# First feed-forward lifted from the unscaled h, S5 parameters moved, 64-row scores in the NSA attention

## The reference

```python
def first_block(...):
    for l in range(DEPTH):
        h = h + hybrid_mixer(rms_norm(h, norm_mix[l]), ...)
        h = h + memory_cross_attention(rms_norm(h, norm_xattn[l]), mem, ...)
    return rms_norm(h, norm_final)          # x * rsqrt(mean(x * x) + eps) * g

def second_block(x, ...):
    h = x
    h = h + 0.5 * _swiglu(_rmsnorm(h, ffn1_norm[0]), ffn1_w_in[0], ffn1_w_out[0])
    ...                                     # S5, feed-forward, kv, feed-forward
    logits = q @ k * 64 ** -0.5 + bias      # NSA: 16 heads of 64, per head and branch
```

## Time and profile before

| | us |
|---|---|
| median of 3 runs | 1496.9 (1495.55 to 1497.25) |
| the profiled execution | 1496.62 |
| its span, first to last instruction | 1494.9 |
| PE busy | 1412.1 (94%) |
| VectorE busy | 845.7 (57%) |
| ScalarE busy | 808.2 (54%) |
| GpSimd busy | 327.3 (22%) |
| chain that ended last | 83% PE, 7% VectorE, 4% ScalarE, 3% GpSimd |

### The profile page before, as it was taken

How to read it: one execution, slowest core, us unless ns; L and a number is a source line. 1 busy time by engine, 2 the same in 40 slices (tenths; PEclk the granted TensorE clock), 3 DMA queues, 4 the chain that set the end, 5 groups by cost and what they waited for, 6 DMA issues and landing times.

```text
span 1494.9 us, 21758 instructions
## 1 busy us (share of the span) xinstructions
PE 1412.1 (94%) x7242; PEld 1165.2 (78%) x7242; DVE 845.7 (57%) x1240; ACT 808.2 (54%) x1322; POOL 327.3 (22%) x369
## 2 busy tenths in 40 slices
PE   7998989999879999958999999999999989999998
PEld 6887878887758887747778888888888875788887
DVE  6537665447566545645665555555555568555553
ACT  7676566665665555322654444765444548464442
POOL 2011000011169979836230000010000015000000
PEclk9999999999989999957999999999999969999999
DMA  9522635513356564210676665577656320355661
GB/s 332 172 91 72 225 128 182 155 58 109 105 145 207 173 176 142 70 29 15 222 245 190 188 187 187 162 146 223 194 182 195 120 71 2 113 183 182 194 185 57
DMA packets 170925, 224.71 MB, mean 150 GB/s; under 512 B 15881, under 2 KB 113393, under 8 KB 170849
## 3 DMA queue, kind: packets, MB, share of 16 engines
q1 hardware_dynamic: 168016, 217.27, 45.8%
q0 software_dynamic: 2160, 6.02, 2.5%
q10 hardware_dynamic: 672, 0.42, 0.1%
HBM read 221.16 MB, written 1.44 MB: 149 GB/s over the span
## 4 chain that ended last, share of the span: by engine, by line
PE 83%; DVE 7%; ACT 4%; POOL 3%; issue 2%; SPq 0%; DMA 0%; ACTq 0%; POOLq 0%; DVEq 0%
PE psum L1611 14%; PE psum L1599 10%; PE psum L1601 10%; PE psum L1600 10%; PE psum L386 8%; PE psum L388 8%; PE psum L387 8%; PE psum L412 2%; PE psum L520 2%; DVE w_lo L338 1%; PE psum L1638 1%; POOL w_raw L2019 1%; PE psum L534 1%; PE psum L2753 1%; ACT w_hi L330 1%
## 5 line engine op out<-in xcount | busy, mean ns | idle before, releaser
L1798 DVE TENSOR_TENSOR w_lo<-w_raw,w_hi 128x1024 fp32r<-128x1024 f32 x216 | 278.3, 1290 | 290.0 <-ACT w_hi L1732 289.8
L1732 ACT ACTIVATE w_hi<-w_raw 128x1024 fp32r<-128x1024 f32 x216 | 228.7, 1060 | 307.4 <-PE psum L1601 216.8
L338 DVE TENSOR_TENSOR w_lo<-w_raw,w_hi 128x1024 fp32r<-128x1024 f32 (+4 forms) x191 | 225.4, 1207 | 121.1 <-ACT w_hi L330 119.6
L1599 PE MATMUL psum<-w_hi,x_hi 128*128 128x512 f32 x704 | 280.9, 399 | 1.5 <-DVE x_lo L438 0.7
L1601 PE MATMUL psum<-w_hi,x_lo 128*128 128x512 f32 x704 | 275.7, 392 | 0.0
L1600 PE MATMUL psum<-w_lo,x_hi 128*128 128x512 f32 x704 | 275.1, 391 | 0.0
L330 ACT ACTIVATE w_hi<-w_raw 128x1024 fp32r<-128x1024 f32 (+4 forms) x191 | 193.3, 1038 | 107.0 <-PE psum L388 61.0
L386 PE MATMUL psum<-w_hi,x_hi 128*128 128x512 f32 (+5 forms) x608 | 232.2, 382 | 3.7 <-DVE x_lo L2886 2.3
L388 PE MATMUL psum<-w_hi,x_lo 128*128 128x512 f32 (+5 forms) x608 | 227.6, 374 | 0.0
L387 PE MATMUL psum<-w_lo,x_hi 128*128 128x512 f32 (+5 forms) x608 | 227.1, 374 | 0.0
L1601 PEld LDWEIGHTS psum<-w_hi,x_lo 128*128 128x128 f32 x704 | 132.7, 188 | 28.6
(11 more groups left out here) (407 smaller groups left out, 1835.4 us busy)
## 6 DMA issues: line engine op xcount, KB each, us to landing
w_raw<-in_ffn_w_in SPq DMA_DIRECT2D x352, 256.0 KB, 3.2
w_raw<-in_ffn_w_out SPq DMA_DIRECT2D x176, 256.0 KB, 2.9
w_raw<-in_w_in SPq DMA_DIRECT2D x88, 256.0 KB, 3.4
w_raw<-in_w_out SPq DMA_DIRECT2D x32, 256.0 KB, 3.8
w_raw<-in_w_kv SPq DMA_DIRECT2D x24, 256.0 KB, 2.9
w_raw<-in_mem_wk SPq DMA_DIRECT2D x16, 256.0 KB, 5.7
w_raw<-in_mem_wv SPq DMA_DIRECT2D x16, 256.0 KB, 4.9
w_raw<-in_mem_wq SPq DMA_DIRECT2D x16, 256.0 KB, 6.6
```

Source lines behind the costliest of these rows:

```text
L338: nc.vector.tensor_tensor(w_lo[:, s, 0:size(u)], w_raw[:, s, 0:size(u)], w_hi[:, s, 0:size(u)].bitcast(F32), ALU.subtract).then_inc(lo_rea ...
L1599: nc.tensor.matmul(o, xh, whi, start=(kt == 0), stop=False)
L1732: nc.scalar.activation(w_hi[:, s, :], w_raw[:, s, :], ACT.Copy).then_inc(hi_ready, 1)
L1798: nc.vector.tensor_tensor(w_lo[:, s, :], w_raw[:, s, :], w_hi[:, s, :].bitcast(F32), ALU.subtract).then_inc(lo_ready, 1)
```

## The change

1. The first feed-forward lifts the unscaled `h`. Its column factor becomes the product of both weights (`norm_final` comes a second time as rows of 8 x 128, is turned by PE and multiplied into `ffn1_norm`), its row factor the product of both `rstd` (`ffn0.scale`). Pairs 0 and 1 are lifted inside `wo1.1`, as soon as the first residual half is there. The final scaling of `h` moves behind the lifts of pairs 2 and 3; the feed-forward's own norm is still taken from the scaled `h`.
2. The S5 activations move to the end of the mixer and the reciprocal to the start of `dve_mem`; GpSimd loads B and C after the values of the memory attention.
3. The NSA scores of a job are two matmuls of 64 rows, one for each head, into the two score banks; the zeros in `kTz` are no longer needed. The compressed scores use the T banks.

```diff
-        nf = area("nf", D)
+        nf = area("nf", D, at=areas["mix"][0])
+        nf_rows = area("nf_rows", P)
...
         def pe_scores(pe, tag, j, job):
-            b = take(pe, "S", f"{tag}.s{j}")
+            banks = [take(pe, "S", x) for x in score_banks(tag, j, job)]
...
+            for i in range(2):
+                o = psum[:, pools["S"][i], 0:job["nk"]] if job["by_rows"] else psum[:, banks[0], i * SEQ:i * SEQ + job["nk"]]
+                last = nc.tensor.matmul(o, job["q"][i], job["k"][i], start=True, stop=True)
...
@@ act_mixer
+            if l == DEPTH - 1:
+                act_s5_params(act)
             for f in range(2):
                 hi_parts(act, chunk_start(f"out{l}.1") + f + 2 + RING)
                 act_lift(act, f"memq{l}", KT, gcol[f"norm_xattn{l}"], pairs=[f])
+            if l == DEPTH - 1:
+                act_s5_params_2(act)
...
@@ pe_mem
+            if l == DEPTH - 1:
+                pe.wait_ge(loads["final"], 32)
+                b = take(pe, "T", "final.gb")
+                nc.tensor.transpose(psum[:, b, 0:KT], nf_rows[0:KT, :], ident[0:KT, 0:KT]).then_inc(*done("lift_pe", "final.gain_turned"))
...
-                for c in range(2):
-                    pe_chunk(pe, f"wo{l}.{c}", tiles_first=None if c else f"mem{l}.olo")
+                pe_chunk(pe, f"wo{l}.0", tiles_first=f"mem{l}.olo")
+                pe_chunk(pe, f"wo{l}.1", after={2: lambda: pe_ffn_lift(pe, 0, [0]), 4: lambda: pe_ffn_lift(pe, 0, [1])})
...
@@ act_mem
-                act_s5_params_2(act)
+                act.wait_ge(*when("final.gain"))
+                for f in range(2):
+                    hi_parts(act, chunk_start(f"wo{l}.1") + f + RING)
+                    act_lift(act, "ffx0", KT, ffn_gain(0), pairs=[f])
+                return
...
@@ dve_mem
+            if l == DEPTH - 1:
+                dve_s5_reciprocal(dve)
...
-                lo_parts(dve, chunk_end(f"wo{l}.0"))
-                dve_s5_reciprocal(dve)
-                dve_residual(dve, f"mem{l}", [f"wo{l}.0", f"wo{l}.1"])
+                def lift_half():
+                    for f in range(2):
+                        lo_parts(dve, chunk_start(f"wo{l}.1") + f + RING)
+                        dve_lift(dve, "ffx0", KT, ffn_gain(0), pairs=[f])
+
+                lo_parts(dve, chunk_end(f"wo{l}.1") + 1)
+                dve.wait_ge(*when("final.gain"))
+                dve_residual(dve, f"mem{l}", [f"wo{l}.0", f"wo{l}.1"], before={1: lift_half}, convert=False)
...
@@ dve_final
-            dve_norm(dve, "final", 20)
             dve.wait_ge(*when("final.rstd"))
-            dve.wait_ge(loads["final"], 16)
+            dve.wait_ge(*when("ffx0.turned3"))
+            dve.wait_ge(loads["final"], 32)
...
@@ act_ffn
-                act_norm(act, f"ffn{f}", i, [FFN_AFTER[f] + ".h11"], [FFN_JUNK[f]])
-                act.wait_ge(*when(f"ffn{f}.rstd"))
+                act_norm(act, f"ffn{f}", i, ["final.h11" if f == 0 else FFN_AFTER[f] + ".h11"], [FFN_JUNK[f]])
+                act.wait_ge(*when("ffn0.scale" if f == 0 else f"ffn{f}.rstd"))
...
@@ dve_ffn
             dve_lift(dve, f"ffx{f}", KT, ffn_gain(f), pairs=range(lifted, KT // 2))
+            if lifted_hook:
+                lifted_hook()
...
+            if f == 0:
+                nc.vector.tensor_tensor(rstd[:, i:i + 2], rstd[:, i:i + 2], rstd[:, 20:22], ALU.mult
+                                        ).then_inc(*done("norm_dve", "ffn0.scale"))
...
@@ pool_s5
-            pool.wait_ge(*when("final.h11"))
+            pool.wait_ge(*when("mem1.sm.pv3"))
...
@@ pool_kv
-            step(nc.gpsimd.memset(kTz, 0.0), "nsa.kTz0")
...
@@ nsa_jobs
-                            q=[qT[:, a, t * P:(t + 1) * P]], k=[kTz[:, NKV * br + a // 2, :, 0:nk]],
+                            q=[qT[HD * i:HD * i + HD, a, t * P:(t + 1) * P] for i in range(2)],
+                            k=[kTz[HD * i:HD * i + HD, NKV * br + a // 2, i, 0:nk] for i in range(2)], by_rows=True,
...
@@ pe_nsa
-                b = take(pe, "S", f"cmp.scores{t}")
+                b = take(pe, "T", f"cmp.scores{t}")
...
@@ sync
+            sp.dma_start(nf_rows[0:KT, :], d["norm_final"].rearrange("(k p) -> k p", p=P)).then_inc(loads["final"], 16)
...
@@ the queues' ends
-            pe_ffn(pe, 0, hooks=...
+            pe_ffn(pe, 0, lifted=2, hooks=...
...
-            dve_final(dve)
-            dve_ffn(dve, 0, hooks=...
+            dve_norm(dve, "final", 20)
+            dve_ffn(dve, 0, lifted=2, lifted_hook=lambda: dve_final(dve), hooks=...
```

More of the change, by code:

```diff
@@ L1491, in dve_mem @@
             dve.wait_ge(*when(f"mem_scale{l}.1"))
+            if l == DEPTH - 1:
+                dve.wait_ge(*when("final.gain_turned"))
+                nc.vector.tensor_tensor(ffn_gain(0), ffn_gain(0), bank("final.gb")[:, 0:KT], ALU.mult
+                                        ).then_inc(*done("norm_dve", "final.gain", frees=("final.gb",)))
             lo_parts(dve, chunk_end(f"wq{l}.0"))
@@ L1767, in act_ffn, with dve_ffn @@
             hi_parts(act, ahead(12))
[L1769 removed]
+        def dve_ffn(dve, f, first=None, early=None, lifted=0, hooks={}, next_lift=None, next_weights=True, in_tail=None, lifted_hook=None):
             u0 = ffn_first[f]
@@ L1776, in dve_ffn @@
                 dve.wait_ge(*when(f"ffn{f}.rstd"))
+            if f == 0:
+                nc.vector.tensor_tensor(rstd[:, i:i + 2], rstd[:, i:i + 2], rstd[:, 20:22], ALU.mult
+                                        ).then_inc(*done("norm_dve", "ffn0.scale"))
+                dve.wait_ge(*when("ffn0.scale"))
             def hidden(c):
```

35 lines of the change are left out of this document (14 added, 21 removed).

## The result

The changed kernel takes 1487.57 us in the median of four runs (1485.51 to 1489.45), the kernel before 1497.08 beside it: 9.5 us less, a ratio of 0.9942, 95% interval 0.9921 to 0.9963. In a second comparison on another chip it was 1486.37 against 1495.23, ratio 0.9930 (0.9908 to 0.9953). The ratios are not the quotients of the medians: by them the change gives 8.7 and 10.5 us, by the medians 9.5 and 8.9. The forecast was 1484.4, 12.5 us less, in a range of 1480.5 to 1490.5. The profiled execution of after took 1487.92, its span is 1486.2.

A forecast was written before the change was run, and what follows sets the result against it. The prediction took the matmul engine, busy for 94% of the span, as the bound. Final norm 7.7 plus scores 4.8 made 12.5 us, so 1496.9 - 12.5 = 1484.4, range 1480.5 to 1490.5.

The forecast's parts named there:

- A delay below 2.6 us is free; 3 us more would pass on: First weights of the next chunk (`u0+4`), beside B and C loads: landing 415.5, needed 418.1; further delay reaches the second residual.
- rival A: Final norm gives only 3 to 4 us of 7.7, through a long dip or late `u0+4`; 1489, chance 0.16.
- The dip: Clock at half speed after PE's 3.2 us gap before the first feed-forward matmuls: loses 1.7 us, bounds none to 2.8.
- The end still moves by 7.7: End of the S5 stage: GpSimd's tables gain only 5.2 us, but its slack lets the end gain the full 7.7.
- that slack: GpSimd's 3.11 us idle for VectorE at the stage's end, 0.6 left after the change; losing it costs up to 1 us.
- Scores: NSA attention, paired 64-row halves: 4.3 us from t = 1, 0.9 from t = 0, less 0.4 at the start; 4.8.
- The estimate from the Trainium skill's page: NSA scores: 1.5 times for two row tiles instead of 1.9, a block of 0.71 and a gain of 3.3 us.
- B: NSA scores: 64-row halves don't pair, so that part gives 0 to -1.5 us; 1489.5, chance 0.15.
- C: NSA scores: 64-row matmuls neither pair nor hide weight loads, +21 us over 32 jobs; 1505, chance 0.05.
- D: Final norm: norm, squares and root bind `f_hid`, PE ends where it was; 1492 with scores only, or 1497; chance 0.04.
- E: Both parts give more: no dip, attention intervals set by ScalarE, 9.4 + 6.2 us; 1481.3, chance 0.10.
- the moved steps: S5 activations and reciprocal in mixer and memory attention: taken as 0, up to 2 us on `memq1` without cover.

The follow-up runs named there:

- e6_params_old: Changed kernel with B and C loads after the second residual half and the second S5 activations and reciprocal back in their old place; 1487.24 us, ratio 0.9946.
- e2_loads_residual: Changed kernel with GpSimd's loads of B and C issued after the second residual half instead of after the memory attention's values; 1484.41 us, ratio 0.9929.
- e11_b_early: Changed kernel with the second residual half ahead of the `u0+4` split and only C's loads moved behind that half, B's left early; 1487.46 us (one run).
- e4_loads_final: Changed kernel with the loads of B and C after the final scaling, as in the kernel before; 1495.26 us, ratio 0.9996.
- e5_residual_first: Changed kernel with B and C loads after the second residual half, and that half ahead of VectorE's `u0+4` split and pair 1 lift; 1485.80 us, ratio 0.9928.
- same rows: Changed kernel with both score matmuls of an NSA job in rows 0 to 63; 1498.78 us, ratio 1.0019.

## Why the prediction was right, and where it was off

The time lay in the range, and the direction and both mechanisms held: the feed-forward starts without the finished norm, and the row halves pair. But the changed places gave 5 to 7 us of the 12.5, and up to 4 came from elsewhere. Without those the time would have been 1490 to 1492, at the edge of the range or beyond it: that the range held is in part luck. Point by point; in the first two points times of after are less the 0.88 us by which it was late at the last `x_lo`, in the others they are those of the trace:

- **Up to the end of wo1.1: right to 0.2 us.** VectorE's splits began at 409.77 (forecast 409.9), the first residual half at 414.13 (414.1), pair 0 was turned at 416.6 (416.7). That the S5 steps left this place is worth 2.9 us (`e6_params_old`).
- **The step that failed: "A delay below 2.6 us is free; 3 us more would pass on".** `u0+4` was some 7 us late: forecast to land at 415.5, it was there at 422.4. So the second residual ended at 426.7 instead of 423.5, the first matmul began at 426.8 instead of 423.6, the scale, `f_hid` and its turn followed 3.1 to 3.2 us late (447.8 instead of 444.6). That is rival A's mechanism, with a chance of 0.16, and the prediction had named its sign: it is wrong if `u0+4` is what ScalarE waits for. That came true. `e2_loads_residual` shows it (without the loads there PE idles 3.08 us and its first matmul is 3.4 us earlier), and `e11_b_early` that B's loads alone bring the wait. I had counted the loads by their share of time and their bytes, and not that beside pieces so small everything comes at less than half the rate. The row was there: 1.03 MB took 84.4% of all engines for 9 us.
- **The clock: right for the gap that was forecast.** The dip was put at 1.7 us behind a gap of 3.2. Behind the 6.44 of after the twelve matmuls of unit 0 took 5.15 us (5.26 in before) instead of 2.8, a loss of 2.4. Behind 3.08 us of idle they took 4.21 (`e2_loads_residual`) and 4.43 (`e4_loads_final`), a loss of 1.4 and 1.6, behind 0.99 (`e5_residual_first`) 2.81, none.
- **"The end still moves by 7.7": wrong by more than the late load.** The turn of `f_hid` gained 4.5 us and the last out units only 1.5. PE now waits 0.63 us for ScalarE's turned S5 parameters (before it came too late to wait), about 0.8 us with the hand-over; a dip at 589.63 behind a gap of 2.13 us cost 1.6, where before has none behind one of 2.38; and the wait for the last `x_lo` at the end grew from 3.95 us to 4.73. There VectorE works on its angles beside GpSimd's tables, and two of its steps, 1.40 and 1.42 us beside GpSimd before, took 1.16 and 1.67, a third 1.53 instead of 0.68. GpSimd's tables began at 449.89, 1.1 us before the 451.02 of the earlier trace rows, where the forecast had them 5.2 earlier, and ended where they had, at 631.3. I had put up to 1 us on that slack; it took 0.8.
- **Scores: 3.6 instead of 4.8.** The pairing is there as taken from the column halves. A block of t = 1 takes 0.64 (forecast 0.58), one of t = 0 0.42 (0.37), and the first transpose behind it comes 0.16 instead of 0.11 before the second. So the period is 1.82 and not 1.71, 1.16 and not 1.14: 3.8 us of 4.3 and 0.7 of 0.9. The start cost 0.9 instead of 0.4: ahead of the first turn PE now waits 1.23, 0.61 and 3.03 us for VectorE's `x` before scores 1, 2 and 3, since each of these jobs takes both banks, and no longer the 0.66, 0.95 and 2.02 us of before. The estimate from the Trainium skill's page ("TensorE: Matmul & The Clock Gate", Part 3, Measured speedup vs the span model), a block of 0.71, was too high by about as much as mine was too low; same rows against two halves is 1.06/0.64 = 1.66 times, its estimate was 1.5.
- **Rivals.** A, with a chance of 0.16, is what happened around the norm: its delay (7 us, it asked for 5), its dip (as long as that of before to 0.1 us), and less than the 3 to 4 us it left of the 7.7 (1.5 to 1.9). Its time was 1489. B and C are refuted by the rows; D is by the turn of `f_hid`, 4.5 us earlier; E did not occur. For the moved steps, put at nothing, no cost shows.

A's price had been carried into the range; what kept the time 3 to 4 us inside it was the stretch behind the first feed-forward, of which the forecast said nothing.

## What to carry to other kernels

Before a load is moved to an earlier place, look not at its bytes but at the size of its pieces and at who queues weights behind it: half a megabyte in pieces of 256 bytes was free here, and another half in pieces of 64 bytes held the weights up by 4 us. When a chain is shortened, each side job that was hidden behind it comes due in turn: here the loads of B and C, then the padding of C (3.1 us). A gain in the profile of one stage is not yet one of the kernel: 3 to 7 us at the end of the first feed-forward never showed in the time here. Two matmuls with half of the rows each paid here only side by side, in different halves and banks.

## What the runs showed of the hardware that I had not expected

- Half a megabyte of loads in pieces of 64 bytes, beside weights: 114 GB/s for all queues together at a DMA share of 0.79, against 258 at 0.84 with pieces of 256 bytes beside the same weights.
- 64-row pairs in float32 stream 256 columns in 0.22 us but start 0.32 apart. The Trainium skill ("TensorE: Matmul & The Clock Gate", Step-by-step: what each phase is for) says that a weight load is pulled ahead of running matmuls if its rows don't conflict or if it goes to the background buffer. In before the load for the first transpose starts with the second score instruction, 0.43 us ahead of its matmul (1250.77 and 1251.19); in after it starts with the matmul itself (1252.43), so at this place it was not pulled ahead. The mark of it, 0.3 us from the last pair to the transpose, is the same in the same rows (1251.38 and 1251.68). Why was not tried.
- The longer gap does not always bring the dip: behind 2.38 us of idle at 592.60 in before the matmuls ran at full speed, behind 2.13 us at 589.63 in after they did not.
